# One decoder layer on one core: prompt choice, sample scores and time steps in one block, and a reworked first norm

## The chip, the core and the metric

The kernel runs on one NeuronCore of a Trainium2 chip. TensorE (PE) multiplies, VectorE (DVE), ScalarE (ACT) and GpSimd (POOL) work element by element, SyncE (SP) and the other queues issue transfers (DMA). All data is float32. The metric is device microseconds of one execution; lower is better.

## The reference, cut to what matters

One inference step of one decoder layer for 256 prompt tokens and 8 sample tokens (one new token each, 1,024 past positions). The two groups share all weights, so most products have 264 columns.

1. x is normed (RMSNorm over 1,024 channels) and multiplied with one input matrix. Its columns give z (2,048), x/B/C (4,096), the time steps dt (32), q, k, v, the indexer's queries, key and weights, and two gates of 1,024.
2. x/B/C goes through a causal convolution of width 4 and SiLU, and then, with dt, through a chunked state-space scan (prompt) or one recurrent step (samples). `dt = softplus(dt_raw + bias)`, `A = -exp(a_log)`.
3. The indexer scores every earlier position, `sum_h w_h relu(q_h k)`, and each query keeps the best: 64 of 256 in the prompt, 256 of 1,025 for a sample. Attention with a relative bias runs over those.
4. Both branches are gated, projected and added to x; then a product-key expert layer (PEER) follows, which picks 128 single-neuron experts for each token and gathers their rows.

## The kernel before

The input projection is cut into 81 tiles of 128 output channels. `Projection.multiply` computes one: eight pairs of multiplications of a 128x128 piece of weights with 264 columns of the normed x (`xn`), so 16 on PE. `Projection.load` issues the weights of tile n (512 KB) into one of `WSLOTS = 4` buffers on SP's queue, `evacuate` takes the result out of one of two PSUM banks on ACT, `convolve` (DVE) does the convolution of an x/B/C tile two tiles later, `tails` (POOL) keeps its last rows. The tiles are dealt out to the blocks that follow each other, to fill PE beside other work. A block ends when all engines have ended their part of it; then semaphores are cleared behind a barrier. The order is written out by hand, and each engine follows its own list. In time order:

- `norm_in` (lines 96 to 141) loads x, the constants (`cst`, `cx`: identity, ones, masks, epsilon), the norm's weights and four weight tiles, all on SP. ACT squares x, PE sums over channels with a matrix of ones from `cst`, ACT takes the root, DVE inverts it and writes `xn` in eight products.
- `project_attention` computes tiles 0 to 16 (q, k, v, indexer, dt); POOL loads 36 of the samples' 64 pages of indexer keys.
- `prepare_attention` norms q and k, builds the bias table, turns v; 6 tiles lie beside it. SP stores `o_k` and waits for the store.
- `choose_prompt` scores the prompt (16 steps: PE, then ReLU on ACT, then a weighted sum on DVE) and finds the best 64 by eight rounds of MAX8 and MATCH_REPLACE8 on two score tiles; 8 tiles beside it, the last 4 with nothing else on PE.
- `score_sample` scores the samples: PE copies queries out, DVE puts them on a diagonal (`iqd`), PE turns the pages and multiplies, ACT copies and rectifies, PE weighs, DVE copies to `negs`. No tile lies beside it.
- `attend_prompt` has 32 steps of prompt attention; in each, DVE also does one round of the samples' choice (MAX8 and MATCH_REPLACE8 over 1,025 scores). 38 tiles lie beside it: z tiles 14 and 15, all 32 x/B/C tiles and 4 gates. So six steps carry two tiles.
- `time_steps` computes dt, its decays and `ex` (values spread to channels by 16 multiplications with a 1 MB matrix `spread`); 2 tiles.
- `attend_sample` runs the samples' attention and the recurrent states (`SampleState`: 1 MB loaded and stored for each sample). The key phase has 16 visits; in each of the first 12 PE turns pages, multiplies, and spreads B and C (`ss_pb`, `ss_pc`) for DVE's update of half a state. Then comes the softmax, and the value phase with two visits for each sample. `LastGates` multiplies the last 10 gate tiles, with three weight buffers of its own and one PSUM bank: two ahead of the softmax, eight in the value phase, one for each sample.
- Then `ssd_chunk` twice, `merge` and `peer`, which the change leaves alone.

Of the kernel before, what the change touches and what calls it, by code (L numbers as in the profile page):

```python
# [19 lines left out]
P = 128  # L20
# [5 lines left out]
T = TP + TS  # L26
# [22 lines left out]
Z0 = N_ATT + 1  # L49
XBC0 = Z0 + N_Z  # L50
GATE0 = XBC0 + N_XBC
N_LAST = 10
# [10 lines left out]
CX_N = 256  # L63
# [8 lines left out]
class Kept:  # L72
# [5 lines left out]
            "d_relbh", "d_spread", "d_state", "d_uv", "d_w_ab", "d_w_in", "d_w_out", "d_wq", "d_xT")  # L78
# [15 lines left out]


def norm_in(nc, k):

    with ExitStack() as ctx:
        sem = signals(nc, ctx)
        xsq, g1, rms = tensors(nc, ctx, n1_xsq=(P, KD, T), n1_g=(P, KD), n1_rms=(P, T))  # L100
        ps = ctx.enter_context(nc.psum_tensor("n1_ps", [P, 512], F32))
        x_loaded, c_loaded, squared, summed, rooted, inverted, done = (sem(n) for n in (
            "n1_x", "n1_c", "n1_sq", "n1_sum", "n1_root", "n1_inv", "n1_done"))
        block = ctx.enter_context(nc.Block())

        @block.sync
        def _(sp):
            sp.dma_start(k.xT[:], k.d_xT[:]).then_inc(x_loaded, 16)
            sp.dma_start(k.cst[:], k.d_cst[:]).then_inc(c_loaded, 16)
            sp.dma_start(k.cx[:], k.d_cx[:]).then_inc(c_loaded, 16)  # L110
            sp.dma_start(g1[:], k.d_g1[:]).then_inc(c_loaded, 16)
            for n in range(WSLOTS):
                k.proj.load(sp, n)
            sp.wait_ge(c_loaded, 48)

        @block.scalar
        def _(act):
            act.wait_ge(x_loaded, 16)
            act.activation(xsq[:], k.xT[:], ACT.Square).then_inc(squared, 1)
            act.wait_ge(c_loaded, 48)  # L120
            act.wait_ge(summed, 1)
            act.activation(rms[:], ps[:, 0:T], ACT.Sqrt, scale=1.0 / D_MODEL, bias=k.eps).then_inc(rooted, 1)

        @block.tensor
        def _(pe):
            pe.wait_ge(c_loaded, 48)
            pe.wait_ge(squared, 1)
            for c in range(KD):
                mm = pe.matmul(ps[:, 0:T], k.ones, xsq[:, c, :], start=c == 0, stop=c == KD - 1)
            mm.then_inc(summed, 1)  # L130

        @block.vector
        def _(dve):
            dve.wait_ge(rooted, 1)
            dve.reciprocal(rms[:], rms[:]).then_inc(inverted, 1)
            dve.wait_ge(inverted, 1)
            dve.wait_ge(c_loaded, 48)
            for c in range(KD):
                dve.scalar_tensor_tensor(out=k.xn[:, c, :], in0=k.xT[:, c, :], scalar=g1[:, c:c + 1],
                                         in1=rms[:], op0=ALU.mult, op1=ALU.mult).then_inc(done, 1)  # L140
            dve.wait_ge(done, KD)


class Projection:
# [30 lines left out]
    def multiply(self, pe, n):  # L175
# [4 lines left out]
        for c in range(KD):  # L180
            mm = pe.matmul(self.ps[:, n % BANKS, 0:T], self.w[:, n % WSLOTS, c * P:(c + 1) * P],  # L181
                           self.k.xn[:, c, :], start=c == 0, stop=c == KD - 1)
        mm.then_inc(self.multiplied, 1)

    def evacuate(self, act, n):
# [3 lines left out]
        if n < XBC0:  # L189
            act.activation(k.zs[:, n - Z0, :], ps, ACT.Silu).then_inc(self.evacuated, 1)  # L190
        elif n < GATE0:
            s = (n - XBC0) % WSLOTS
            if n - XBC0 >= WSLOTS:

                act.wait_ge(self.convolved, n - XBC0 - WSLOTS + 1)
                act.wait_ge(self.saved, n - XBC0 - WSLOTS + 1)
# [5 lines left out]
        i = n - WSLOTS - XBC0  # L202
        if 0 <= i < KC:
# [3 lines left out]
    def convolve(self, dve, n):  # L207

        i = n - 2 - XBC0
        if not 0 <= i < KC:  # L210
            return
        s, cv = i % WSLOTS, self.cv[:, i % WSLOTS, :]

        dve.wait_ge(self.evacuated, i + XBC0 + 1)
# [15 lines left out]
    def tails(self, pool, n):  # L230

        i = n - XBC0
        if not 0 <= i < KC:
            return
        s = i % WSLOTS
# [64 lines left out]
def project_attention(nc, k):  # L300


    with ExitStack() as ctx:
        sem = signals(nc, ctx, "pr_")
        table, = (sem("table"),)
        block = ctx.enter_context(nc.Block())
# [3 lines left out]
        def _(sp):  # L310
            with sp.Fori(1, N_ATT // WSLOTS) as i:
# [5 lines left out]
            for n in range(N_ATT, Z0 + WSLOTS):  # L317
                pj.load(sp, n)

        @block.tensor  # L320
        def _(pe):
            for n in range(WSLOTS):
                pj.multiply(pe, n)
# [12 lines left out]
        def _(act):  # L336
            act.dma_start(pj.cw[:], k.d_cw[:]).then_inc(pj.c_loaded, 16)
# [4 lines left out]
            act.dma_start(k.hot[:], k.d_hot[:]).then_inc(k.tables_loaded, 16)  # L342
            with act.Fori(0, N_ATT // WSLOTS) as i:
# [6 lines left out]
            act.wait_ge(pj.evacuated, N_ATT + 1)  # L350

# [9 lines left out]
def prepare_attention(nc, k, tiles):  # L361

    with ExitStack() as ctx:
# [7 lines left out]
         stored, doubled, copied_table) = (sem("pa_" + n) for n in (  # L371
             "sq", "sum", "root", "inv", "normed", "turned", "copied", "tab", "tabout", "spread",
             "stored", "dup", "tabcp"))
# [5 lines left out]
        def _(sp):  # L379
            sp.dma_start(k.ikd[0:HD, :], k.misc[0:HD, :]).then_inc(doubled, 16)  # L380
            sp.dma_start(k.ikd[HD:P, :], k.misc[0:HD, :]).then_inc(doubled, 16)
            sp.dma_start(k.o_ik[:], k.misc[0:HD, :]).then_inc(stored, 16)
            sp.dma_start(k.o_v[:], k.att[:, V0:V0 + 2, :]).then_inc(stored, 16)
# [12 lines left out]
            sp.dma_start(k.o_k[:], k.att[:, K0:K0 + 2, :]).then_inc(stored, 16)  # L396
            sp.wait_ge(spread, 16)
            sp.wait_ge(doubled, 32)
            sp.wait_ge(stored, 48)
# [75 lines left out]
def choose_prompt(nc, k, tiles):  # L475

    TAIL = 4
    with ExitStack() as ctx:
        sem = signals(nc, ctx)
        r, iw = tensors(nc, ctx, cp_r=(P, 4, TP), cp_iw=(P, 2, IH))  # L480
        score, = tensors(nc, ctx, cp_score=(P, 2, TP))
        top, = tensors(nc, ctx, cp_top=(P, 2, 8))
        ps = ctx.enter_context(nc.psum_tensor("cp_ps", [P, 4, 512], F32))
        weighed, multiplied, rectified, added, cut, found, replaced, masked, final = (sem("cp_" + n) for n in (
            "w", "mm", "relu", "add", "cut", "max", "rep", "mask", "final"))
        block = ctx.enter_context(nc.Block())
        steps = [(i, h) for i in range(2) for h in range(IH)]
        width = lambda i: P * (i + 1)

        share, tail = shares(tiles[:-TAIL], len(steps)), tiles[-TAIL:]  # L490

# [6 lines left out]
        def _(pe):  # L498
# [9 lines left out]
            for tile in tail:  # L508
                k.proj.multiply(pe, tile)

        @block.scalar
        def _(act):
# [9 lines left out]
            for tile in tail:  # L522
                k.proj.evacuate(act, tile)

        @block.vector
        def _(dve):
            dve.tensor_scalar(iw[:], k.mnat[:, :, IW_P:IW_P + IH], IH ** -0.5, None, ALU.mult).then_inc(weighed, 1)
# [14 lines left out]
            for step in range(SEL_P // 8):  # L542
                for i in range(2):
# [8 lines left out]
                    dve.match_replace(s, top[:, i, :], s, LOW).then_inc(replaced, 1)  # L552
            for i in range(2):
# [3 lines left out]
            for tile in tail:  # L557
                k.proj.convolve(dve, tile)

        @block.gpsimd  # L560
        def _(pool):
            for tile in tiles:
                k.proj.tails(pool, tile)
            for i in range(2):
# [4 lines left out]
                                   pattern=[[-1, P]], channel_multiplier=1).then_inc(cut, 1)  # L569
            for i in range(2):  # L570
# [5 lines left out]


def score_sample(nc, k):

    with ExitStack() as ctx:  # L580
        sem = signals(nc, ctx, "cs_")
        ikt, iqd, r, wsel = tensors(
            nc, ctx, cs_ikt=(P, 2, 512), cs_iqd=(P, TS, TS * IH), cs_r=(TS * IH, NKS),
            cs_wsel=(TS * IH, TS))
        tr = ctx.enter_context(nc.psum_tensor("cs_tr", [P, 2, 512], F32))
        small = ctx.enter_context(nc.psum_tensor("cs_small", [P, 512], F32))
        ps = ctx.enter_context(nc.psum_tensor("cs_ps", [P, 3, 512], F32))
        cleared, spread, diag, weighed, turned, copied, scored, rectified, summed, read = (sem(n) for n in (
            "clr", "spread", "diag", "w", "turn", "copy", "score", "relu", "sum", "read"))
        block = ctx.enter_context(nc.Block())  # L590

        ik = k.paged[:].rearrange("p (a d) -> p a d", d=HD)

        @block.tensor
        def _(pe):

            for h in range(IH):
                pe.matmul(small[:, h * TS:(h + 1) * TS], k.selhi if h % 2 else k.sello,
                               k.att[:, IQ0 + h // 2, TP:T], start=True, stop=True)
# [1662 lines left out]
```

## Time and profile before

| what | us |
|---|---|
| median of 3 runs (lowest to highest) | 1476.19 (1475.57 to 1476.94) |
| the profiled execution's own time; its span | 1481.15; 1479.5 |
| `norm_in`, to the first projection tile | 0 to 22.9 |
| `project_attention` | 22.9 to 86.4 |
| `prepare_attention` | 86.4 to 124.25 |
| `choose_prompt` and `score_sample` | 124.25 to 186.3 |
| `attend_prompt` | 186.3 to 379.2 |
| `time_steps` | 379.2 to 399.2 |
| `attend_sample` | 399.2 to 548.3 |
| the rest | 548.3 to 1479.5 |

The times of blocks are read from the trace; each begins with its first instruction. In the rows below, a group of the timeline begins with its start and its duration (us), then engine, line, operation, output<-inputs, forms and how often; the bracket holds the idle time of that engine before it and what ended it. A row marked x16 covers a run of 16 instructions. A row of the windows view holds the stretch, its length, the busy time of PE, PEld (loads of weights into PE), DVE, ACT and POOL with their instructions in brackets, PEclk (the granted TensorE clock as a share of full speed), the busy share of the DMA engines and the GB/s that they moved.

### The profile page before, as it was taken

To read this page: it belongs to the slowest core of one execution; us is meant where nothing else is said; L and a number is where in the kernel's file an instruction comes from. 1 tells how busy PE (TensorE), PEld (TensorE's weight loads), DVE (VectorE), ACT (ScalarE), POOL (GpSimd) and SP (SyncE) were. 2 spreads that over 40 slices of the span, in tenths; PEclk is the share of its full clock that TensorE was granted. 3 is DMA by queue.
4 is the path that set the end of the run, shared out by engine and by line. 5 is a ranking of instruction groups with operands and counts; after the bars stand their busy time and mean duration, and the time that the engine had idled before them with its cause. 6 is when DMAs were issued, how large, how long until landed. Compare 5 with 4: busy or idle time off the path is not lost. (4 is left out here: it accounts for less than half of the span.)

```text
span 1479.5 us, 17316 instructions
## 1 busy us (share of the span) xinstructions
PE 1257.2 (85%) x4988; PEld 770.5 (52%) x4988; DVE 857.2 (58%) x2345; ACT 580.8 (39%) x1542; POOL 383.9 (26%) x510
## 2 busy tenths in 40 slices
PE   5997899999677878889989999877778777777776
PEld 4876578777555557758867555322223222222221
DVE  1044369998284334551116867878965667776444
ACT  1153237878383404320004444343343333333343
POOL 1320012222021110010002445443534334333341
PEclk8998999999796889899999999999999999999999
DMA  4563123334289462123337999999999999999995
GB/s 151 172 214 99 58 93 122 111 103 148 100 285 327 149 232 76 29 72 117 112 127 297 420 421 421 421 420 421 421 422 421 421 421 420 421 421 419 421 413 238
DMA packets 80185, 391.26 MB, mean 264 GB/s; under 512 B 13432, under 2 KB 23192, under 8 KB 43744
## 3 DMA queue, kind: packets, MB, share of 16 engines
q0 software_dynamic: 43104, 287.92, 47.5%
q1 hardware_dynamic: 36016, 100.68, 19.9%
q10 hardware_dynamic: 976, 1.61, 0.3%
q8 instruction: 39, 0.64, 0.2%
q14 instruction: 50, 0.41, 0.1%
HBM read 378.43 MB, written 11.60 MB: 264 GB/s over the span
## 5 line engine op out<-in xcount | busy, mean ns | idle before, releaser
L2039 DVE CUSTOM_DVE_ANT_0 pe_uv<-pe_uv,pe_hnat 128x1024 f32<-128x1024 f32 x264 | 322.9, 1223 | 195.4 <-DMA pe_uv<-d_uv,pe_idx 180.5
L1899 POOL DMA_INDIRECT pe_uv<-d_uv,pe_idx x256 | 268.0, 1047 | 398.4 <-PE pe_acc L1776 184.3
L1776 PE MATMUL pe_ph<-pe_uv,pe_dg 128*128 128x512 f32 x512 | 253.0, 618 | 69.8 <-ACT pe_dg L1843 69.8
L1776 PE MATMUL pe_acc<-pe_uv,pe_dg 128*128 128x512 f32 (+1 forms) x544 | 257.8, 610 | 49.3 <-ACT pe_dg L1843 49.3
L181 PE MATMUL pi_ps<-xn,pi_w 128*128 128x264 f32 x944 | 228.3, 399 | 9.5 <-PEq L87 9.5
L1776 PEld LDWEIGHTS pe_ph<-pe_uv,pe_dg 128*128 128x128 f32 x512 | 87.0, 189 | 235.3 <-ACT pe_dg L1843 173.1
L181 PEld LDWEIGHTS pi_ps<-xn,pi_w 128*128 128x128 f32 x944 | 183.5, 198 | 42.8 <-issue 11.3
L1837 ACT ACTIVATE pe_gl<-pe_a 128x1 f32<-128x1 f32 x264 | 53.4, 202 | 379.0 <-DVE pe_a L2039 378.5
L1776 PEld LDWEIGHTS pe_acc<-pe_uv,pe_dg 128*128 128x128 f32 (+1 forms) x544 | 93.7, 184 | 205.0 <-ACT pe_dg L1843 118.2
L1843 ACT ACTIVATE pe_dg<-cst,pe_w 128x128 f32<-128x128 f32 x256 | 102.7, 401 | 8.3
L1840 ACT ACTIVATE pe_w<-pe_gl,pe_gw 128x1 f32<-128x1 f32 x256 | 75.4, 295 | 8.3
L1715 PE MATMUL pq_ps<-hN,pq_w 128*128 128x264 f32 x256 | 61.7, 399 | 6.4 <-DMA pq_w<-d_wq 6.4
L957 PE MATMUL mg_pa<-Y,mw_w 128*128 128x264 f32 x256 | 60.5, 401 | 0.0
L1715 PEld LDWEIGHTS pq_ps<-hN,pq_w 128*128 128x128 f32 x256 | 50.1, 197 | 19.1 <-DMA pq_w<-d_wq 6.8
L957 PEld LDWEIGHTS mg_pa<-Y,mw_w 128*128 128x128 f32 x256 | 50.5, 198 | 10.1 <-issue 1.0
L226 DVE SCALAR_TENSOR_TENSOR pi_cv<-pi_raw,pi_cw,pi_cv 128x288 f32<-128x288 f32 x96 | 49.8, 519 | 3.4
L1260 DVE SCALAR_TENSOR_TENSOR ss_h<-ss_pb,ss_dtx,ss_h 128x128 f32<-128x128 f32 x128 | 35.0, 343 | 24.9 <-ACT ss_h L1247 17.0
L1617 ACT ACTIVATE mg_sq<-xT 128x264 f32<-128x264 f32 x8 | 3.4, 423 | 109.4 <-DVE xT L1647 109.4
L244 POOL COPY pi_tail_p<-pi_raw 128x3 f32<-128x3 f32 x32 | 12.0, 374 | 132.1 <-ACT pi_raw L198 132.1
L330 PE MATMUL pi_ps<-xn,pi_w 128*128 128x264 f32 x192 | 42.9, 386 | 0.0
L296 POOL DMA_DIRECT2D paged<-d_cik x50 | 26.8, 536 | 58.2 <-issue 58.2
L276 PE MATMUL lg_ps<-xn,lg_w 128*128 128x264 f32 x160 | 40.0, 406 | 1.7 <-DMA lg_w<-d_w_in 1.1
(296 smaller groups left out, 1655.9 us busy)
## 6 DMA issues: line engine op xcount, KB each, us to landing
pi_w<-d_w_in SPq DMA_DIRECT2D x71, 512.0 KB, 3.5
mw_w<-d_w_ab SPq DMA_DIRECT2D x24, 512.0 KB, 3.7
ss_h<-d_state SPq DMA_DIRECT2D x8, 1024.0 KB, 6.9
o_ssm_s<-ss_h SPq DMA_DIRECT2D x8, 1024.0 KB, 7.0
pq_w<-d_wq SPq DMA_DIRECT2D x16, 512.0 KB, 7.7
paged<-d_ck POOLq DMA_DIRECT2D x40, 128.0 KB, 3.3
lg_w<-d_w_in SPq DMA_DIRECT2D x10, 512.0 KB, 6.4
paged<-d_cv POOLq DMA_DIRECT2D x32, 128.0 KB, 4.9
```

What stands on the lines that cost most here:

```text
L181: mm = pe.matmul(self.ps[:, n % BANKS, 0:T], self.w[:, n % WSLOTS, c * P:(c + 1) * P], self.k.xn[:, c, :], start=c == 0, stop=c == KD - 1)
L226: dve.scalar_tensor_tensor(out=cv, in0=self.raw[:, s, j:j + CV], scalar=self.cw[:, i, j:j + 1], in1=cv, op0=ALU.mult, op1=ALU.add).then_in ...
L276: mm = pe.matmul(self.ps[:, 0:T], self.w[:, s, c * P:(c + 1) * P], self.k.xn[:, c, :], start=c == 0, stop=c == KD - 1)
L330: mm = pe.matmul(pj.ps[:, s % BANKS, 0:T], pj.w[:, s, c * P:(c + 1) * P], k.xn[:, c, :], start=c == 0, stop=c == KD - 1)
L957: mm = pe.matmul(out, self.w[:, i % self.RING, c * P:(c + 1) * P], rhs(c), start=c == 0 and piece < 2, stop=c == KD - 1 and piece != 1)
L1715: mm = pe.matmul(qps[:, n % BANKS, 0:T], w[:, n % WSLOTS, c * P:(c + 1) * P], k.hN[:, c, :], start=c == 0, stop=c == KD - 1)
L1776: mm = pe.matmul(accs[n][0:m, 4 * half:4 * half + 4, :], lhsT, uv[:, r, D_MODEL + half * 512:D_MODEL + (half + 1) * 512], start=False, sto ...
L1837: act.activation(gl[:, r:r + 1], a[:, r:r + 1], ACT.Gelu_apprx_tanh).then_inc(gelued, 1)
L1840: act.activation(wt[:, r:r + 1], gl[:, r:r + 1], ACT.Copy, scale=g).then_inc(weighed, 1)
L1843: act.activation(out, mask, ACT.Copy, scale=wt[:, r:r + 1]).then_inc(diagonal, 1)
L1899: pool.indirect_dma_start(uv[:, r, :], None, k.d_uv[:], bass.IndirectOffsetOnAxis(ap=src, axis=0)).then_inc(gathered[r], 16)
L2039: dve.tensor_tensor_reduce(uv[:, r, 0:D_MODEL], uv[:, r, 0:D_MODEL], hnat[:, n, :], 1.0, 0.0, ALU.mult, ALU.add, a[:, r:r + 1]).then_inc(d ...
```

## The change

`norm_in` goes into `project_attention`. x comes in four parts, which DVE squares as they come; the ones are written on chip; ACT loads the square root's table early; `cx` and the norm's weights come on ACT's queue, and `cst` on SP's behind the first four weight tiles. The first tile's multiplications wait for `xn` piece by piece.

`choose_prompt`, `score_sample` and `time_steps` become one block, `choose`, with 7 tiles. The time steps' parts and the samples' diagonal lie between the rounds of the prompt's choice on DVE; `ex` comes from one multiplication with a small selection matrix in place of 16. Their inputs are loaded in `prepare_attention`, scratch space lies in the not yet written `gate`.

The tiles are dealt out anew: z and x/B/C in the order `COLUMNS`; 7 tiles in `prepare_attention` (before 6), 7 in `choose` (8, and 2 in `time_steps`), 34 in `attend_prompt` (38), one for each step and two behind, and 16 in `LastGates` (10): one behind each of the key phase's visits 3, 6, 9 and 12, two ahead of the softmax, ten in the value phase (two at the first and the fifth sample). The bias inputs of `attend_sample` are loaded in `attend_prompt`. The wait for the stores of `prepare_attention` goes to `attend_prompt`.

```diff
-N_LAST = 10
+N_LAST, N_KEYS = 16, 4
+COLUMNS = "z" * 7 + "x" * 4 + "z" * 3 + "x" * 28 + "z" * 6
...
 def project_attention(nc, k):
...
         def _(sp):
+            for i in range(PARTS):
+                sp.dma_start(k.xT[:, i * WIDE:(i + 1) * WIDE, :], k.d_xT[:, i * WIDE:(i + 1) * WIDE, :]
+                             ).then_inc(x_loaded[i], 16)
+            for n in range(WSLOTS):
+                pj.load(sp, n)
+            sp.dma_start(k.cst[:], k.d_cst[:]).then_inc(c_loaded, 16)
...
         def _(pe):
+            pe.wait_ge(filled, 1)
+            for c in range(KD):
+                if c % WIDE == 0:
+                    pe.wait_ge(squared, c // WIDE + 1)
+                mm = pe.matmul(sums[:, 0:T], one[:], xsq[:, c, :], start=c == 0, stop=c == KD - 1)
             for n in range(WSLOTS):
-                pj.multiply(pe, n)
+                pj.multiply(pe, n, (lambda c: pe.wait_ge(done, c + 1)) if n == 0 else None)
...
         def _(act):
+            act.dma_start(k.cx[:], k.d_cx[:]).then_inc(eps_loaded, 16)
+            act.dma_start(g1[:], k.d_g1[:]).then_inc(eps_loaded, 16)
+            act.wait_ge(filled, 2)
+            act.activation(warm[:, 1:2], warm[:, 0:1], ACT.Sqrt).then_inc(warmed, 1)
...
 def prepare_attention(nc, k, tiles):
...
+            sp.dma_start(k.ts["bias"], k.d_dtb[:]).then_inc(k.steps_loaded, 16)
+            sp.dma_start(k.ts["alog"], k.d_alog[:]).then_inc(k.steps_loaded, 16)
+            sp.dma_start(k.dskip[:], k.d_dskip[:]).then_inc(k.steps_loaded, 16)
...
-            sp.wait_ge(stored, 48)
...
+def choose(nc, k, tiles):
+    TAIL, STEPS = 3, SEL_P // 8
...
         def _(pe):
...
+            k.proj.multiply(pe, tail[0])
+            pe.wait_ge(rectified, len(steps))
...
+            k.proj.multiply(pe, tail[1])
...
+                if b == 1:
+                    pe.wait_ge(diag, TS)
+                if b:
+                    scores(b - 1)
+                if b == 5:
+                    pe.wait_ge(s_weighed, 2)
+                    pe.wait_ge(dA_ready, 1)
...
+            k.proj.multiply(pe, tail[2])
...
         def _(act):
...
+            act.wait_ge(abs_ready, 1)
+            act.activation(e, a, ACT.Exp, scale=-1.0).then_inc(e_ready, 1)
+            act.wait_ge(k.steps_loaded, 48)
+            act.activation(alog, alog, ACT.Exp).then_inc(alog_ready, 1)
+            k.proj.evacuate(act, tail[0])
+            act.wait_ge(u_ready, 1)
+            act.activation(l, u, ACT.Ln).then_inc(log_ready, 1)
+            k.proj.evacuate(act, tail[1])
+            for b in range(TS):
...
+                if b == 4:
+                    act.wait_ge(dA_ready, 1)
+                    act.activation(both[rows, TS:2 * TS], k.dA[rows, NP_:ALL], ACT.Exp).then_inc(both_dA, 1)
...
         def _(dve):
...
+            for step in range(STEPS):
...
+                for tile in beside[step]:
+                    k.proj.convolve(dve, tile)
+                if step == 1:
...
+                    dve.tensor_tensor(e, a, e, ALU.mult).then_inc(ratio, 1)
+                if step == 4:
+                    dve.wait_ge(spread, 1)
+                    for b in range(TS):
...
 def attend_prompt(nc, k, tiles):
...
-        share = shares(tiles, N) + [[]] * LAG_O
+        share = shares(tiles[:-2], N) + [[], tiles[-2:-1], tiles[-1:]]
...
+            sp.dma_start(k.as_hot, k.d_hots[:]).then_inc(k.bias_loaded, 16)
+            sp.dma_start(k.as_rel, k.d_relbh[:]).then_inc(k.bias_loaded, 16)
...
 def attend_sample(nc, k):
...
-        after = [[]] * VK + [[0, 1]] + shares(range(2, N_LAST), TS)
+        after = ([[(t - 3) // 3] if t % 3 == 0 and 3 <= t < 3 + 3 * N_KEYS else [] for t in range(VK)]
+                 + [[N_KEYS, N_KEYS + 1]] + shares(range(N_KEYS + 2, N_LAST), TS))
...
+                if visit - NG < gates.SLOTS:
+                    gates.load(sp, visit - NG)
...
-        weights_at = [VK + NG + 1 if t == VK else VK + NG + 2 * (t - VK) for t in turn]
+        weights_at = [t + NG + 1 if t <= VK else VK + NG + 2 * (t - VK) for t in turn]
...
                 if n % 2 == 1 and n // 2 < EARLY:
                     ssd.spread(pe, n // 2)
+                if n % 2 == 1 and n // 2 < VK:
+                    for g in after[n // 2]:
+                        gates.multiply(pe, g)
...
-        ends = [Z0, Z0 + 6, Z0 + 14, END - BANKS, END]
+        ends = [FIRST0, FIRST0 + 7, FIRST0 + 14, END]
```

## Rows read from the trace of the kernel before

**Rows 1.** Stages by windows view: us, busy us of each engine, PEclk, DMA share, GB/s:
```profile
124.25:186.30 62.05, 56.29 (x264) 39.53 (x264) 20.66 (x81) 14.42 (x36) 1.16 (x4) 0.89 0.21 68
...
186.30:379.20 192.90, 188.47 (x880) 149.91 (x880) 165.61 (x385) 139.04 (x290) 40.70 (x112) 0.98 0.34 112
...
379.20:399.20 20.00, 15.37 (x68) 13.34 (x68) 3.74 (x15) 7.54 (x13) 0.00 (x0) 0.76 0.18 57
...
399.20:477.60 78.40, 55.29 (x524) 41.46 (x524) 47.93 (x306) 45.45 (x128) 17.16 (x32) 0.78 0.88 314
```

**Rows 2.** Timeline of the start:
```profile
5.92 1.96 ACT L119 ACTIVATE n_xsq<-xT 128x2112 f32<-128x2112 f32 x1 [3.74 <-DMA xT<-d_xT]
...
8.03 6.80 PE L129 MATMUL n_ps<-n_xsq,cst 128*128 128x264 f32 x16 [8.03 <-ACT n_xsq L119]
...
14.92 1.28 ACT L122 ACT_TABLE_LOAD   x1 [7.03 <-PE n_ps L129]
...
16.73 1.80 DVE L135 RECIPROCAL n_rms<-n_rms 128x264 f32<-128x264 f32 x1 [16.73 <-ACT n_rms L122]
...
18.57 3.32 DVE L139 SCALAR_TENSOR_TENSOR xn<-xT,n_g,n_rms 128x264 f32<-128x264 f32 x8
...
22.86 7.33 PE L181 MATMUL pi_ps<-xn,pi_w 128*128 128x264 f32 x21 [8.03 <-PEq L87]
```

**Rows 3.** Timeline, one of 13 projection tiles that repeat: ACT's copy behind each:
```profile
43.45 0.39 ACT L346 ACTIVATE att<-pi_ps 128x264 f32 x1 [3.17 <-PE pi_ps L330]
```

**Rows 4.** SP's own waits at the end of `prepare_attention`: us, times, longest:
```profile
SPq L399 <- DMA o_k<-att: 1.7, 1, 1.7
```

**Rows 5.** Timeline of `choose_prompt` and `score_sample`:
```profile
147.85 0.28 DVE L550 MAX8 cp_top<-cp_score 128x8 f32<-128x128 f32 x1
...
159.42 0.42 DVE L555 TENSOR_SCALAR negp<-cp_score 128x128 f32<-128x128 f32 x2
...
166.87 1.97 PE L611 MATMUL cs_ps<-cs_ikt,cs_iqd 64*64 64x512 f32 x4
...
180.62 0.22 PE L613 MATMUL cs_ps<-misc,cs_iqd 64*64 64x1 f32 x2
...
184.01 1.34 DVE L661 COPY negs<-cs_ps 8x512 f32<-8x512 f32 x3 [18.90 <-PE cs_ps L631]
```

**Rows 6.** Timeline of `attend_prompt`: two steps of its first half, and the end:
```profile
227.65 0.41 DVE L222 TENSOR_SCALAR pi_cv<-pi_raw,pi_cw,pi_cb 128x288 f32<-128x288 f32 x1
...
228.09 1.63 DVE L226 SCALAR_TENSOR_TENSOR pi_cv<-pi_raw,pi_cw,pi_cv 128x288 f32<-128x288 f32 x3
...
228.19 0.48 PE L721 MATMUL ap_psl<-att 64*128 64x128 f32 x2
...
232.87 0.41 DVE L222 TENSOR_SCALAR pi_cv<-pi_raw,pi_cw,pi_cb 128x288 f32<-128x288 f32 x1
...
232.92 0.49 PE L721 MATMUL ap_psl<-att 64*128 64x128 f32 x2
...
375.87 2.05 PE L742 MATMUL ap_pso<-ap_pt,vnat 128*128 128x128 f32 x8 [3.10 <-ACT ap_pt L805]
```

**Rows 7.** Waits in the key phase of `attend_sample`: us, times, longest:
```profile
PE as_tr L1403 <- DMA paged<-d_ck: 6.6, 2, 3.7
...
ACT ss_h L1247 <- DMA ss_h<-d_state: 5.6, 2, 3.8
...
PE as_pl L1379 <- DMA as_rel<-d_relbh: 4.5, 1, 4.5
```

**Rows 8.** Timeline of one visit of the key phase:
```profile
412.79 0.65 PE L1237 MATMUL ss_pc<-cst,xbc 128*128 128x128 f32 x4 [0.96 <-DVE ss_y L1268]
```

**Rows 9.** Timeline of the value phase: two gates:
```profile
498.66 3.80 PE L276 MATMUL lg_ps<-xn,lg_w 128*128 128x264 f32 x16
...
505.55 3.83 PE L276 MATMUL lg_ps<-xn,lg_w 128*128 128x264 f32 x16 [1.08 <-DMA lg_w<-d_w_in]
```

**Rows 10.** Waits in the value phase:
```profile
PE as_pl L1437 <- DMA paged<-d_cv: 3.1, 2, 2.5
```

More of the change, by code:

```diff
@@ L93, in signals @@
     return sem
[L96 to L141, printed above, removed]
 class Projection:
@@ L230, in tails @@
     def tails(self, pool, n):
[L232 to L233 removed]
+        if n not in X_AT:
             return
+        i = X_AT[n]
         s = i % WSLOTS
@@ L305, in project_attention @@
         table, = (sem("table"),)
+        xsq, g1, rms, one, warm = tensors(nc, ctx, n1_xsq=(P, KD, T), n1_g=(P, KD), n1_rms=(P, T), n1_one=(P, P),
+                                          n1_warm=(P, 2))
+        sums = ctx.enter_context(nc.psum_tensor("n1_ps", [P, 512], F32))
+        PARTS, WIDE = 4, KD // 4
+        x_loaded = [sem(f"n1_x{i}") for i in range(PARTS)]
+        c_loaded, eps_loaded, squared, summed, rooted, inverted, done, filled, warmed = (sem("n1_" + n) for n in (
+            "c", "eps", "sq", "sum", "root", "inv", "done", "one", "warm"))
         block = ctx.enter_context(nc.Block())
@@ L350, in _ @@
             act.wait_ge(pj.evacuated, N_ATT + 1)
+        @block.vector
+        def _(dve):
+            dve.memset(one[:], 1.0).then_inc(filled, 1)
+            dve.memset(warm[:], 1.0).then_inc(filled, 1)
+            for i in range(PARTS):
+                dve.wait_ge(x_loaded[i], 16)
+                xi = k.xT[:, i * WIDE:(i + 1) * WIDE, :]
+                dve.tensor_tensor(xsq[:, i * WIDE:(i + 1) * WIDE, :], xi, xi, ALU.mult).then_inc(squared, 1)
+            dve.wait_ge(rooted, 1)
+            dve.reciprocal(rms[:], rms[:]).then_inc(inverted, 1)
+            dve.wait_ge(inverted, 1)
+            dve.wait_ge(eps_loaded, 32)
+            for c in range(KD):
+                dve.scalar_tensor_tensor(out=k.xn[:, c, :], in0=k.xT[:, c, :], scalar=g1[:, c:c + 1],
+                                         in1=rms[:], op0=ALU.mult, op1=ALU.mult).then_inc(done, 1)
         @block.gpsimd
@@ L483, in choose_prompt @@
         ps = ctx.enter_context(nc.psum_tensor("cp_ps", [P, 4, 512], F32))
+        tr = ctx.enter_context(nc.psum_tensor("cs_tr", [P, 2, 512], F32))
+        small, cum, px = ps[:, 3, 0:256], ps[:, 3, 256:256 + 2 * NP_], tr[:, 0, 0:KI * 2 * TS]
         weighed, multiplied, rectified, added, cut, found, replaced, masked, final = (sem("cp_" + n) for n in (
             "w", "mm", "relu", "add", "cut", "max", "rep", "mask", "final"))
+        cleared, spread, diag, s_weighed, turned, copied, scored, s_rectified, summed, read = (
+            sem("cs_" + n) for n in ("clr", "spread", "diag", "w", "turn", "copy", "score", "relu", "sum", "read"))
@@ L486, in choose_prompt @@
+        x_ready, abs_ready, e_ready, alog_ready, u_ready, rest, inverted, ratio, log_ready = (
+            sem("ts_" + n) for n in ("x", "abs", "e", "alog", "u", "rest", "inv", "ratio", "log"))
+        log_out, dt_ready, dA_ready, both_dt, both_dA, each_ready, cumulated, widened, nac_ready, seg_ready, dec_exp, \
+            etot_ready, last = (sem("ts_" + n) for n in (
+                "lout", "dt", "dA", "bdt", "bdA", "each", "cum", "wide", "nac", "seg", "dexp", "etot", "last"))
         block = ctx.enter_context(nc.Block())
+        rows = slice(DT_P, P)
@@ L507, in _ @@
                     k.proj.multiply(pe, tile)
-            for tile in tail:
-                k.proj.multiply(pe, tile)
+            k.proj.multiply(pe, tail[0])
+            pe.wait_ge(rectified, len(steps))
+            for h in range(IH):
+                pe.matmul(small[:, h * TS:(h + 1) * TS], k.selhi if h % 2 else k.sello,
+                          k.att[:, IQ0 + h // 2, TP:T], start=True, stop=True)
+            pe.matmul(small[0:TS * IH, 128:128 + TS], k.iwsel, k.misc[:, TP:T], start=True, stop=True
+                      ).then_inc(spread, 1)
@@ L511, in _ @@
+            k.proj.multiply(pe, tail[2])
+            pe.wait_ge(s_rectified, 1)
+            for at, n in ((0, 512), (512, 512), (1024, 1)):
+                mm = pe.matmul(ps[0:TS, at // 512, 0:n], wsel[:], sr[:, at:at + n], start=True, stop=True)
+            mm.then_inc(summed, 1)
+            pe.wait_ge(each_ready, 1)
+            pe.matmul(px, k.half_of, k.ts["each"][rows, :], start=True, stop=True,
+                      tile_position=(DT_P, 0)).then_inc(widened, 1)
         @block.scalar
@@ L783, in _ @@
                     k.proj.convolve(dve, tile)
+            assert not any(t - 2 in X_AT for t in tiles[-2:])
             dve.wait_ge(replaced, N)
@@ L1462, in _ @@
                     ssd.fade(act, n // 2)
+                if n % 2 == 0 and n:
+                    for g in after[n // 2 - 1]:
+                        gates.evacuate(act, g)
             for g in after[VK]:
```

387 lines of the change are left out of this document (166 added, 221 removed).

## Prediction, made before the changed kernel ran

> **What bounds the kernel now.** I read the windows by stage first. Nothing after `attend_sample` is touched, so only the 548 us before it matter, and each stage there has its own limit. In `attend_prompt` PE is busy 188.5 of 192.9 us at a clock of 0.98, so a tile taken out of it is worth a tile. `time_steps` works 15.4 of its 20 us on PE, two tiles and a chain of small steps behind them. The key phase of `attend_sample` keeps the DMA engines 88% busy and PE only 55.3 of 78.4 us [rows 1]. Then I read the timeline of the start: the norm is one chain from engine to engine, and the first tile begins at 22.86 [rows 2]. A tile costs 3.56 us at the full clock (0.39 of copy and 3.17 of waiting between two copies) [rows 3]. Last came the waits, since the change moves stores, weights and tiles behind other waits [rows 4, 7, 10].
>
> The number of tiles stays 81. So a gain can only come from idle PE time, and the sum is taken along the chain of blocks: how much earlier or later does each one end than it would?
>
> **The start.** Before: the sum over channels begins at 8.03 and takes 6.80, the table load 1.28, root and hand-over 0.5, inversion 1.84, eight products 3.32, the barrier 0.97 [rows 2]. After, a quarter of x can be squared while the rest comes. All of x took until 5.92. A part's square is priced from the products, 0.415 for 264 columns, so 0.83 for 528. PE can begin between 3.0 (a quarter of the 5 us from issue to landing, plus 0.83) and 6.8 (all of x, plus 0.83); I take 4.5. Then 6.80 again for the sum, 0.1 + 0.5 + 1.84, and one product of 0.42, since PE follows piece by piece: the first tile begins at 14.2, which is 8.7 earlier (bounds 6.4 to 10.2). The constants behind the weights cost nothing: `cst` is first read 17 tiles or 60 us later; the weights that take its place in the queue have until 14.2, and what stood in that place before had landed by 8.0, or PE could not have begun. If that cover went, the first tile would wait for its weights. POOL's page loads and ACT's loads start earlier and have the same 60 us.
>
> The 1.28 of the table load is in this sum as the row has it. The Trainium skill, "ScalarE: Activation LUTs", section "What ACT_TABLE_LOAD costs", says that a change of table set costs about 2.66 us, 1.28 for the load and 1.38 for a drain. The row shows no drain: load and root end within 1.9 us of the load's beginning. By the page the start would gain 1.4 more, by the row it does not, and I stay with the row.
>
> **`prepare_attention`.** One more tile, 3.56; the wait for the store of `o_k`, 1.7 [rows 4], goes: 1.9 later (bounds 0.5, if the tile fills a wait of PE, and 3.6). The three added loads on SP stand ahead of the bias table's trip to memory; next late would be the weights of the fifth tile, and those wait for the first tile anyway.
>
> **`choose`.** Before, 62.05 + 20.0 = 82.05 [rows 1]. Up to the last prompt score nothing moves on PE (the same four tiles lie between), so DVE starts the rounds at 147.85 again, and eight rounds take 11.57, 1.45 each [rows 5]. The samples' diagonal now waits for five rounds (7.2), two convolutions (2.07 each, begin of the first to end of the last step [rows 6]) and four small steps of the time steps (1.4, estimated from 15 such in 3.74 us of DVE time [rows 1]); with 0.9 for the diagonal that is 161.4. PE has by then done two tiles and turned two pages and stands, at about 157.5, for 4 us. From the first sample score to the last took 166.87 to 180.84, 14.0 [rows 5]; begun at 161.4 it ends at 175.4, plus 1.5 for the cumulative sums and a table change on ACT in the middle, plus the last tile 3.56 (which hides ACT's rectifying, about 1.2 of the 3.2 between 180.84 and the copies at 184.01), plus 1.9 for the weighing: 182.4. From the copies' start to the next block took 186.3 - 184.0 = 2.3, and `ex` adds 0.4: 185.1. That is 1.2 earlier, and the 20.0 are gone: 21.2. Bounds: 16, if ACT's four further table changes at 1.28 all fall into the path; 25, if PE keeps its full clock through the 4 us (the first pages then go as fast as the last) and the diagonal comes a round earlier.
>
> **`attend_prompt`.** Four tiles fewer: 14.2. Against it stands DVE: in the first half PE's step takes 4.73 (228.19 to 232.92), DVE's step with a convolution 5.22 (227.65 to 232.87) [rows 6], and from the third step on each of 14 steps has one. That is 6.9 us in all, of which PE's two buffers hide some; between 0 and 6.9 I take 3.5. The two last tiles lie where PE waited 3.1 for ACT at the end [rows 6], which gives that back. The two bias loads at the head of SP's queue delay weights that are four tiles ahead, so nothing: -14.2 + 3.5 - 3.1 = -13.8 (bounds -17.3 and -7.3).
>
> **`attend_sample`** takes six more tiles, 21.4 on PE. Begin: PE no longer waits 4.5 for the bias inputs [rows 7], but the diagonal of queries and the first state come at their own time; between 0 and 4.5 I take 2.0. Key phase: a gate behind `ss_pc` fills the 0.96 that PE waits there [rows 8] and delays DVE by the rest, 2.6; three of them 7.8, the fourth lies in the 6.6 of waiting for pages. The delay is given back where states come late anyway, 5.6 [rows 7]. Their weights, 2.1 MB, are 6.7 us at 314 GB/s, against 12% of 78.4 = 9.4 us of idle DMA [rows 1]; I take 2 of it as lateness. Three of these loads go from SP's visits 13 to 15 to 4 to 6, and each later one waits on SP for the gate three before it, with pages and states queued behind; that gate is done by then, since SP comes to the visit only when PE has turned pages behind it. That is -2.0 + 7.8 - 5.6 + 2 = +2.2. Value phase: the second gate of the first sample is wanted at 502.4, when the first ends, but its weights are issued where those were that PE waited 1.08 for and got at 505.55 [rows 9]: 3.1 of waiting, less the 1.08. SP comes to those weights only when both visits of that sample are mixed, so this can't be earlier. Two more tiles 7.1, less 3.1 of waiting for pages that they fill [rows 10]: +6.0. In all 8.2 (bounds -0.5, which is the whole 4.5 at the begin, nothing for the key phase and 4.0 for the value phase; +24.5, with six whole tiles and the 3.1).
>
> **The sum.** -8.7 + 1.9 - 21.2 - 13.8 + 8.2 = -33.6. The profiled execution took 1481.15, so 1447.5 for such a one; the median lies 4.96 lower, at 1476.19, so 1442.6.
>
> **Rivals.**
> (a) The gates are paid in full. For it: in the key phase every engine waits for a chain through two buffers, and SP issues states, pages and gates in one order. Against it: 5.6 + 6.6 us of DMA waits lie there. `attend_sample` +24.5 in place of +8.2: 1458.9.
> (b) More goes: the full clock holds in `choose` (-3), PE's buffers hide DVE's pace (-3.5), and denser work in `attend_sample` saves part of the stretches at half clock that hold its clock at 0.78 (-4). Each has a row for it [rows 1, 6]; all together are less likely: 1432.
> (c) The start does not do what it says: x or the weights land so late in parts that nothing is gained, 1451.3. Against it: PE and DVE work in series there before, and the barrier goes in any case.
> (d) The other side: PE falls to the lower of its two clock levels in the first half of `attend_prompt`, since DVE now sets the pace and PE stops in each step. The same 16 multiplications took 6.80 in the norm and 3.56 later, so a tile would cost 3.24 more [rows 2, 3]: 16 tiles 52, 1495; it decides from ten tiles on. The Trainium skill, "TensorE: Matmul & The Clock Gate", section "A second HAM failure mode: psum-queue depth-cycling", says just this of a kernel whose matmul groups are parted by short waits on PSUM. Here the rows speak against it: PE would still be busy 4.73 of 5.22 us, and the clock was low where PE was busy 70% of the time, not at 98% [rows 1].
>
> **Chances and range.** Forecast 0.60, (a) 0.18, (b) 0.12, (c) 0.06, (d) 0.04. About 0.2% (3 us) is what a measurement can tell from no change: faster 0.96; of (d) one part in four ends near zero, same 0.01; slower 0.03. The range runs from 1430 to 1459: it holds the forecast's own bounds, nearly all of (c), half of (a) and two thirds of (b).
>
> **What would show it.** The first tile near 14.2; the block after `choose` some 21 us nearer to the end of `prepare_attention` than `attend_prompt` and `attend_sample` together were; `attend_prompt` near 179 us, with steps near 5.2 in its first half; the key phase 2 us longer, the value phase 6. The prediction is wrong if PE's clock falls outside the waits named, if ACT's table changes in `choose` hold up the pages, or if states and pages in the key phase come later by more than the gates take.

## The result, and the profile after

The changed kernel takes 1430.03 us (median of 4 runs, 1427.50 to 1433.12), before 1476.57 (4 runs): ratio 0.9677, 95% interval [0.9642, 0.9711]. On the median of the table above that is 1428.5, so 47.7 less where 33.6 were forecast; it lies just below the range. The profiled execution took 1433.12 with a span of 1431.5, so the span fell by 48.0.

To see where, I took the borders of the stages from the timelines. The first column is the forecast, the second the two profiled executions, the third means over three profiles a side: before, b1 and b2 below against after, b3 and b4, which differ from them in places of tiles and one small load (for the last row only the two of each side whose ring of expert rows lies where it lay).

| stage | forecast | profiled pair | means |
|---|---|---|---|
| start and `project_attention` | -8.7 | -7.8 | -8.1 |
| `prepare_attention` | +1.9 | 0.0 | +1.7 |
| `choose`, `attend_prompt` | -35.0 | -35.7 | -34.3 |
| `attend_sample`, key phase | +2.2 | -3.9 | -4.3 |
| softmax and value phase | +6.0 | +13.0 | +9.9 |
| `ssd_chunk` to the first gather | 0 | -3.5 | -0.1 |
| from the first gather to the end | 0 | -10.1 | -10.1 |
| sum | -33.6 | -48.0 | -45.3 |

Up to the first gather the means give -35.2, close to the forecast, though the two halves of `attend_sample` miss in opposite ways. The rest is the last row, in `peer`, which no line of the diff touches.

Windows of the kernel after, by stage (columns as in [rows 1]): `choose`, `attend_prompt`, key phase, softmax and value phase, and the gathers.

```profile
116.49:176.16 59.67, 52.76 (x254) 36.56 (x255) 32.17 (x114) 22.70 (x54) 3.44 (x16) 0.92 0.20 63
176.16:355.73 179.57, 176.27 (x816) 136.71 (x816) 157.54 (x369) 132.31 (x277) 37.50 (x100) 0.99 0.32 104
355.73:430.05 74.32, 60.45 (x588) 47.71 (x589) 48.26 (x306) 47.47 (x133) 16.78 (x32) 0.95 0.93 332
430.05:514.02 83.97, 67.31 (x383) 48.17 (x382) 22.66 (x116) 19.37 (x53) 13.27 (x25) 0.90 0.54 183
...
751.00:1387.60 636.60, 535.67 (x1308) 223.63 (x1306) 457.50 (x1167) 255.18 (x797) 270.61 (x255) 0.99 1.01 424
```

The same windows view of the kernel before, from its first gather to its 256th:

```profile
788.90:1434.90 646.00, 535.05 (x1308) 221.98 (x1306) 457.81 (x1167) 255.38 (x797) 267.07 (x256) 1.00 1.01 419
```

The engines do the same work in both; the DMA engines are busy throughout (1.01), and move 424 GB/s in place of 419. `attend_prompt` kept its clock, and the key phase, which had 0.78 [rows 1], has 0.95.

Timeline of the start after (answers to [rows 2]):

```profile
4.10 1.46 DVE L344 TENSOR_TENSOR n_xsq<-xT 128x528 f32<-128x528 f32 x2 [2.92 <-DMA xT<-d_xT]
...
4.95 6.43 PE L298 MATMUL n_ps<-n_xsq,n_one 128*128 128x264 f32 x16 [4.95 <-DVE n_xsq L344]
...
7.25 0.71 DVE L344 TENSOR_TENSOR n_xsq<-xT 128x528 f32<-128x528 f32 x1 [0.54 <-DMA xT<-d_xT]
...
11.48 0.48 ACT L327 ACTIVATE n_rms<-n_ps,cx 128x264 f32<-128x264 f32 x1 [8.15 <-PE n_ps L298]
...
14.47 2.10 PE L139 MATMUL pi_ps<-xn,pi_w 128*128 128x264 f32 x4 [3.09 <-DVE xn L350]
```

PE's sum begins at 4.95 while the last part of x is squared only at 7.25, and the first tile begins at 14.47 (forecast 14.2).

### The profile page after: what moved, and what is told of

Its sections match the earlier page's. It is cut to its first block and busy times, and to the rows that moved or that the text cites. A ratio compares the mean times of both kernels' runs of the same rounds, so it can differ in the third digit from the quotient of the medians.

```text
span 1431.5 us, 17196 instructions
## 1 busy us (share of the span) xinstructions
PE 1239.8 (87%) x4958; PEld 755.6 (53%) x4958; DVE 859.9 (60%) x2353; ACT 577.3 (40%) x1542; POOL 386.1 (27%) x510
## 3 DMA queue, kind: packets, MB, share of 16 engines
q0 software_dynamic: 43104, 287.92, 48.4%
## 5 line engine op out<-in xcount | busy, mean ns | idle before, releaser
L1878 POOL DMA_INDIRECT pe_uv<-d_uv,pe_idx x256 | 271.6, 1061 | 385.0 <-PE pe_ph L1755 178.6
L139 PE MATMUL pi_ps<-xn,pi_w 128*128 128x264 f32 x848 | 205.2, 398 | 3.1 <-DVE xn L350 3.1
L139 PEld LDWEIGHTS pi_ps<-xn,pi_w 128*128 128x128 f32 x848 | 163.1, 196 | 32.0 <-issue 4.7
L234 PE MATMUL lg_ps<-xn,lg_w 128*128 128x264 f32 x256 | 65.3, 411 | 7.8 <-DMA lg_w<-d_w_in 6.6
L234 PEld LDWEIGHTS lg_ps<-xn,lg_w 128*128 128x128 f32 x256 | 50.6, 203 | 20.0 <-DMA lg_w<-d_w_in 8.3
L202 POOL COPY pi_tail_p<-pi_raw 128x3 f32<-128x3 f32 x32 | 6.8, 212 | 138.2 <-ACT pi_raw L156 138.2
```

Source lines behind the costliest of these rows:

```text
L234: mm = pe.matmul(self.ps[:, 0:T], self.w[:, s, c * P:(c + 1) * P], self.k.xn[:, c, :], start=c == 0, stop=c == KD - 1)
L1878: pool.indirect_dma_start(uv[:, r, :], None, k.d_uv[:], bass.IndirectOffsetOnAxis(ap=src, axis=0)).then_inc(gathered[r], 16)
```

## Experiments

Every ratio is to the kernel before on the same chip. Without an edit of its own, a kernel is the changed one.

**b1 to b4: the gathers.** `CX_N` goes from 256 to 272 in the diff. `cx` lives to the end, so all that is allocated behind it moves by 64 bytes in each partition: the ring of expert rows `pe_uv` goes from byte 110,272 to 110,336. b1 is the kernel before, unchanged; the others:

```diff
# b2, in the kernel before
-CX_N = 256
+CX_N = 272
# b3, in peer
-        uv, hnat, ... = tensors(nc, ctx, pe_uv=(P, RING, 2 * D_MODEL), ...
+        _, uv, hnat, ... = tensors(nc, ctx, pe_pad=(P, 16), pe_uv=(P, RING, 2 * D_MODEL), ...
# b4, in prepare_attention, and d_spread among the inputs
+            sp.dma_start(k.spare[:], k.d_spread[:, 0:16]).then_inc(k.steps_loaded, 16)
```

> The kernel before, unchanged. The part behind attend_sample took 931.2 us in its profiled execution and 917.5 in that of the changed kernel, though no line of it differs: about 2.4 in the two ssd blocks, 1.2 up to the first gather and 9.4 in the gathers of the expert rows (646.0 against 636.6 us from the first to the last of 256, 421 against 427 GB/s). Theory 'execution': the gathers' rate differs from one execution to the next whatever the kernel, so this one lies anywhere between 636 and 646 us. Theories 'ring' and 'table' (the place of the ring in SBUF, the place of the expert table in DRAM): 646 again, within 2.

> The kernel before with one constant changed: the table cx is 272 columns wide in place of 256, its new columns zero and unread. All that is allocated behind it in SBUF, the ring of expert rows included, then lies 64 bytes further, where the changed kernel has it. Theory 'ring': the gathers take about 636.6 us and the kernel about 1466, 0.993 of before. Theories 'table' and 'execution': no difference from before by more than the runs scatter, ratio 1.000, gathers as in the run of the unchanged kernel.

> The changed kernel with 64 unused bytes in each partition ahead of the ring of expert rows, so that the ring lies at the same place relative to 128 bytes as in the kernel before. Theory 'ring': the gathers take 646 us again and the kernel about 1439.5, 0.975 of before. Theories 'table' and 'execution': as the changed kernel, about 1430, 0.968.

> The changed kernel with the input d_spread (1 MB) put back among its inputs; only 8 KB of it are loaded, into a tile of 64 bytes a partition that nobody reads, beside the other small loads of prepare_attention. Theory 'table': the expert table lies where it lay before, the gathers take 646 us again and the kernel about 1439.5, 0.975 of before. Theories 'ring' and 'execution': about 1430, 0.968; the tile lies in SBUF that the ring later covers, so the ring's place is unchanged.

Measured: b1 0.9987 [0.9973, 1.0001], b2 0.9926 [0.9901, 0.9951], b3 0.9734 [0.9713, 0.9756], b4 0.9687 [0.9664, 0.9710]. The gathers in the view of the ring's tile (duration of one in ns, lowest, median and highest; first and last start), in b2, b3 and the changed kernel:

```profile
L1899 POOL DMA_INDIRECT pe_uv<-d_uv,pe_idx x256: 942/944/3291, 783.7 to 1421.2; - x128
```
```profile
L1878 POOL DMA_INDIRECT pe_uv<-d_uv,pe_idx x256: 942/947/3337, 751.7 to 1397.3; - x128
```
```profile
L1878 POOL DMA_INDIRECT pe_uv<-d_uv,pe_idx x256: 939/944/3299, 751.0 to 1387.6; - x128
```

So 637.5, 645.6 and 636.6 us; b1 took 646.0 and b4 636.7. A wider table in the old kernel takes the gain, a pad in the new one gives it back, and the 1 MB input does nothing: theory "ring". The pad of b3 moves the tiles allocated behind the ring by 64 bytes too; no run moved the ring alone, but 265.6 of the 270.7 MB of the stretch before lie on the gathers' queue.

**c1 to c4: parts of the change.**

```diff
# c1
-N_LAST, N_KEYS = 16, 4
+N_LAST, N_KEYS = 14, 4
# c2
+N_LAST, N_KEYS = 12, 0
# c3
-        PARTS, WIDE = 4, KD // 4
+        PARTS, WIDE = 1, KD
# c4, in choose: the diagonal (DVE), the sums (PE), the exponent (ACT)
-                if step == 4:
+                if step == 1:
-                if b == 5:
+                if b == 7:
-                if b == 4:
+                if b == 6:
```

> The changed kernel with two gate tiles moved back from the value phase to attend_prompt (14 last gates in place of 16; no sample has two any more, two of 32 steps carry two tiles again). Theory 'late weights': the value phase is 9.9 us longer than before in the mean of three profiles each, though its two more tiles are only 7.5 of multiplication; the rest is the second gate of the first sample, which waits 3.7 for its weights and then runs at the lower clock (6.9 in place of 3.8), and later gates whose weights come late in turn. Then the value phase falls by 9 to 13, attend_prompt grows by 7.1, and the kernel takes 2 to 6 us less than the changed one. Rival 'a tile is a tile': the value phase falls by 7.5, attend_prompt grows by 7.1, and the time is that of the changed kernel within 1 us.

0.9649 [0.9617, 0.9681], 1425.2 us. The interval overlaps that of the changed kernel, so I read the stages (d2, below, is clear of it in time). The value phase fell by 13.8 (83.97 to 70.2), `attend_prompt` grew by 6.9. PE in the value phase of the changed kernel, and then of c1:

```profile
450.69 3.73 PE L234 MATMUL lg_ps<-xn,lg_w 128*128 128x264 f32 x16
458.08 6.86 PE L234 MATMUL lg_ps<-xn,lg_w 128*128 128x264 f32 x16 [3.67 <-DMA lg_w<-d_w_in]
```
```profile
457.98 3.73 PE L234 MATMUL lg_ps<-xn,lg_w 128*128 128x264 f32 x16
461.63 1.06 PE L1413 MATMUL as_pl<-paged,as_pt 128*16 128x256 f32 x16
```

The second gate of the first sample is gone, and its wait and its slow run with it: "late weights".

> The changed kernel without gates in the key phase: 12 last gates, four more tiles in attend_prompt. Theory 'hidden': in the key phase the four gates lie in waits for states and pages, so it stays at 73 to 74 us from the first bias product to the end of the last score product, within 2; attend_prompt grows by 4 x 3.55 = 14.2, and the kernel takes 12 to 16 us more than the changed one. The prediction's size for the key phase (each gate delays VectorE by 2.6, and 5.6 of the 7.8 are given back): it falls by some 4 us with its lateness of weights, so 10 more. Rival (a), the gates are paid in full: it falls by 15, the time does not change.

0.9735 [0.9703, 0.9767], 1436.33 us. The key phase took 66.1, so four gates cost 7.4 (against the mean of three profiles) to 8.2 (against the changed kernel's) of their 14.9 on PE; they are neither hidden nor paid in full. This is one profile, and the ten kernels that have the four gates took between 71 and 76 there, so the cost is known only to some 2 us. `attend_prompt` grew by 11.2, not 14.2.

> The changed kernel with x loaded in one transfer and squared in one instruction. Theory 'parts': about half of the 8 us that the start gained comes from squaring behind the first part; all of x takes until about 6, one square of 2112 columns 3.3, so TensorE's sum begins at 9.3 in place of 4.95, and the first tile begins at about 18.5 in place of 14.5: 4 us more. Rival 'weights decide': the first tile waits for its weights behind x anyway, and nothing is lost.

0.9711 [0.9672, 0.9750]. Timeline of c3:

```profile
6.33 2.36 DVE L344 TENSOR_TENSOR n_xsq<-xT 128x2112 f32<-128x2112 f32 x1 [5.15 <-DMA xT<-d_xT]
8.83 5.44 PE L298 MATMUL n_ps<-n_xsq,n_one 128*128 128x264 f32 x16 [8.83 <-DVE n_xsq L344]
```

PE's sum begins 3.9 later and takes 1.0 less, since it no longer waits for parts; the root begins at 14.38 against 11.48, and the first tile at 17.37 against 14.47. The parts are worth 2.9 of the start's 8; the time alone could not show it.

> The changed kernel with the samples' diagonal on VectorE behind the second round of the prompt's choice in place of the fifth, and the two waits for the time steps two samples later in the loop of sample scores. Theory 'on the path': TensorE stands 4.5 us for that diagonal (from 149.0 to 153.55), and the loop of sample scores decides when the block ends; the diagonal is then done at about 147.5, the first scores begin at about 149.5 to 150, and the block ends 3 to 4 us earlier; the kernel takes 3 to 4 us less. Rival 'rounds decide': the block ends with VectorE's rounds and the time steps behind them, and nothing is gained.

0.9667 [0.9629, 0.9704], 1425.03 us; the interval overlaps that of the changed kernel, so here too the stage tells: `choose` took 54.3 in place of 59.67. PE in the changed kernel and in c4, from the samples' first pages to the first scores:

```profile
147.97 1.04 PE L559 MATMUL cs_tr<-cst,paged 128*128 128x128 f32 x8
153.55 1.92 PE L548 MATMUL cp_ps<-cs_ikt,cs_iqd 64*64 64x512 f32 x4 [4.54 <-DVE cs_iqd L676]
```
```profile
145.44 1.04 PE L559 MATMUL cs_tr<-cst,paged 128*128 128x128 f32 x8
147.00 1.08 PE L548 MATMUL cp_ps<-cs_ikt,cs_iqd 64*64 64x512 f32 x4 [0.52 <-ACT cs_ikt L607]
```

The wait for the diagonal is gone (4.0 less between the two rows), and the first products behind it take 1.08 in place of 1.92, at a granted clock of 1.00 in place of 0.52: "on the path".

**d1: where the first gates' weights are loaded.** On top of c2:

```diff
-                if visit - NG < gates.SLOTS:
-                    gates.load(sp, visit - NG)
+                if VK - gates.SLOTS <= visit < VK:
+                    gates.load(sp, visit - VK + gates.SLOTS)
```

> The kernel of c2 (no gates in the key phase, 12 last gates) with the loads of the first three gates' weights back at the visits 13 to 15 where the kernel before had them, in place of 4 to 6. Theory 'place of the weights': without gates the key phase takes 66.1 us from the first state's load to the end of the last score product, 12 less than before (78.1); about 4 of that is its begin (no wait for the bias inputs, bias products at the full clock), and the other 8 come from 1.5 MB of weights that no longer stand between the last pages: before, TensorE waited 2.9 and 3.7 for those pages, fell to the lower clock and did the last products at it. Then the key phase takes 71 to 74 us here, with waits of several us for pages near its end, and the kernel 4 to 8 more than c2. Rival 'begin alone': the whole 12 come from a denser begin that keeps the clock and the transfers going; the key phase stays at 66, within 2.

0.9759 [0.9718, 0.9801], 1442.19 us; the interval overlaps c2's, but the key phase took 72.6 against 66.1. Waits of its key phase, us, times, longest, in c2 and in d1:

```profile
PE as_tr L1376 <- DMA paged<-d_ck: 2.5, 2, 1.9
```
```profile
PE as_tr L1376 <- DMA paged<-d_ck: 5.6, 2, 2.9
```

Windows view of the last 7.5 us of the key phase, in before, d1 and c2:

```profile
470.00:477.60 7.60, 7.60 (x74) 4.90 (x72) 0.00 (x0) 1.19 (x2) 1.07 (x2) 0.50 1.03 360
432.70:440.20 7.50, 6.38 (x78) 4.81 (x78) 0.00 (x0) 1.20 (x2) 1.38 (x3) 0.67 1.03 370
423.40:430.80 7.40, 5.38 (x94) 3.69 (x94) 0.00 (x0) 1.74 (x4) 2.81 (x6) 1.00 0.86 276
```

Before and d1 do their last products at a lowered clock, c2 at the full one. So the place of these weights is worth 6.5 ("place of the weights"; one profile each); 5.2 remain for the begin (77.8, the mean of three profiles of before from the block's first instruction, to 72.6). That is a difference; no run changed the begin alone.

**d2 to e1: both gains together, and which places of the ring are slow.** d2 is c1 and c4 in one. d3, d4 and e1 are d2 with `pe_pad` of 64, 8 and 32 columns.

> The changed kernel with both edits that gained: the diagonal early (c4) and two gates back in attend_prompt (c1). If the two lie in different stages, their gains add: the block choose some 5 us shorter, the value phase 13 shorter and attend_prompt 7 longer, in all 9 to 11 us less than the changed kernel, about 0.961 of before. Rival: what one gains the other takes, as both end in the same late pages or states: 5 to 6 less, as each alone.

> d2 with 256 unused bytes ahead of the ring of expert rows, so that it begins at a multiple of 512 bytes in its partition; in the changed kernel it begins at 256 past such a multiple, in the kernel before at 192 past one. Theory '128': only the place relative to 128 bytes counts, so the gathers take 636.6 us as in d2 and the time is the same. Theory '512': larger multiples help further; the gathers take less than 634 us.

> d2 with 32 unused bytes ahead of the ring, which then begins 32 bytes past a multiple of 64. If each row's 8 KB in a partition is written in pieces that end at multiples of 64 or more, a start that is no multiple of 64 is at least as bad as one at an odd multiple of 64: gathers of 646 us or more, the kernel 9 us or more above d2. If only the odd 64 was bad, 637.

> d2 with 128 unused bytes ahead of the ring of expert rows, which then begins 128 bytes past a multiple of 256. The fast places so far (those of the changed kernel and of d3) are multiples of 256, the slow ones lie 192, 64 and 32 past one, so the runs do not tell which multiple is wanted. Theory '256': the gathers take 645 to 648 us as at the slow places, the kernel some 10 us more than d2. Theory '128': 636.6 as in d2, no difference.

d2: 0.9588 [0.9558, 0.9619], 1417.30 us, faster than both kernels, by ratio 13.1 less than the changed one; `choose` took 54.2 as in c4, and the value phase some 69, about as in c1: the gains add. d3 0.9608 [0.9576, 0.9639], d4 0.9694 [0.9654, 0.9733], e1 0.9656 [0.9604, 0.9708]. The gathers of d4 and of e1:

```profile
L1878 POOL DMA_INDIRECT pe_uv<-d_uv,pe_idx x256: 939/944/3356, 732.0 to 1379.9; - x128
```
```profile
L1878 POOL DMA_INDIRECT pe_uv<-d_uv,pe_idx x256: 939/944/3317, 738.9 to 1384.9; - x128
```

| ring begins, past a multiple of 256 bytes | gathers, us | kernels |
|---|---|---|
| 0 | 636.5 to 637.5 | after, b2, b4, c1 to c4, d1 to d3 |
| 32 | 647.9 | d4 |
| 64 | 645.6 | b3 |
| 128 | 646.0 | e1 |
| 192 | 646.0 | before, b1 |

d4 is slow like the odd 64, and e1 shows that a multiple of 128 is not enough. Of the places tried, those at a multiple of 256 are fast, and a multiple of 512 (d3) adds nothing.

## Why the prediction was right in direction and too small

**The step that failed** is its first: "Nothing after `attend_sample` is touched, so only the 548 us before it matter". The code there is not touched, but its addresses are. The term that it set to nothing measured -10.1 (9.4 to the last of 256 gathers, 0.7 behind it); b2 and b3 show the cause from both sides. With the ring at a slow place again (b3) the changed kernel has 0.9734, which is 1436.9 on the table's median and 39.3 less than before, a time inside the range. What the page of before showed, and I did not weigh, is that the gathers fill the DMA engines for 646 us, so that 1.5% on them is 9.4 us, more than the whole start gives.

That the means up to the first gather give -35.2 is in part luck: the key phase came out 6.5 below its term and the value phase 3.9 above it. It is luck too that rival (b), at 1432, lies nearest to the 1428.5 measured: the key phase apart, its terms did not come. And the range holds the bounds of the terms only one at a time; the low ones taken together are -52.5, or 1423.7.

The Trainium skill, "DMA: Bandwidth & Descriptors", section "How a descriptor splits into AXI transactions", says that a transaction must begin at a multiple of 256 bytes, and that a descriptor which does not begin at one has its first transaction begin at the boundary below. It tells this of what is read; here the place that is written was moved, and the runs show the same 256 there. They do not agree with its count of beats (32 bytes each) as a price: for a row of 8 KB that would be 262 in place of 256 at 192 past (+2.3%) and 257 at 32 past (+0.4%, both estimates by that page); measured were +1.5% and +1.8%. Why the price is nearly the same at every offset stays open.

**Start: right.** -8.1 against -8.7. The table load is gone from the path and the barrier with it; neither was undone alone. As to its price, the timeline of the changed kernel has one in `choose`, with ACT's steps 0.01 ahead of it and behind it:

```profile
138.33 0.94 ACT L590 ACTIVATE gate<-cp_ps 128x256 f32<-128x256 f32 x3 [0.17 <-PE cp_ps L526]
139.28 1.28 ACT L596 ACT_TABLE_LOAD   x1
140.57 0.26 ACT L596 ACTIVATE gate<-gate 128x72 f32<-128x72 f32 x1
```

By the Trainium skill, "ScalarE: Activation LUTs", section "What ACT_TABLE_LOAD costs", 1.38 of drain would come on top; these rows leave no room for it on either side of the load.

**`prepare_attention`: right** in the mean (+1.7 against +1.9), though single profiles of one kernel differ by as much.

**`choose`: right.** -22.4 against -21.2 in the profiled pair. PE stood 4.54 for the diagonal (forecast 4), the loop from there to the last score took 13.95 with the sums in it (15.5), and c4 shows that this wait was on the path. The merging itself was read from the traces, not undone.

**`attend_prompt`: right.** 179.57 (forecast 179). From its eleventh step on DVE sets the pace in the first half; two steps in the timeline:

```profile
240.05 0.48 PE L798 MATMUL ap_psl<-att 64*128 64x128 f32 x2
...
245.28 0.48 PE L798 MATMUL ap_psl<-att 64*128 64x128 f32 x2
```

5.23 a step, as in [rows 6] for DVE. Rival (d) did not come: the granted clock is 0.99 there. What the Trainium skill, "TensorE: Matmul & The Clock Gate", section "A second HAM failure mode: psum-queue depth-cycling", tells of short idle times between groups, cited beside that rival, is not seen in these steps.

**Key phase: two sizes wrong.** The gates cost 7.4 (four at some 2), not 7.8 - 5.6 + 2 = 4.2. Against that I booked 2 for the begin, which gave 5.2 (by difference; the wait of 4.5 [rows 7] is gone, and the bias products, below, take 2.06 in place of 3.99, at a granted clock of 1.00 in place of 0.50), and a loss for moved weights that was a gain of 6.5 (d1): before, 1.5 MB stood between the last pages at the end of the phase, and PE waited there and did its last products at 0.50 of the clock. -5.2 - 6.5 + 7.4 = -4.3, a sum that must come out, as its terms are differences between the same four times. The bias products in the timelines of before and after:

```profile
401.83 3.99 PE L1379 MATMUL as_pl<-as_p,as_rel 32*128 32x512 f32 x6 [4.49 <-DMA as_rel<-d_relbh]
```
```profile
355.77 2.06 PE L1351 MATMUL as_pl<-gate 32*128 32x512 f32 x6 [1.74 <-PEq L91]
```

**Value phase: two sizes too small.** The late second gate was foreseen (3.1; it waited 3.67). Not foreseen was that PE's clock is lowered behind that wait: the gate then took 6.86 in place of 3.83. Windows view over it:

```profile
458.00:464.90 6.90, 6.82 (x20) 5.04 (x23) 0.00 (x0) 0.00 (x0) 0.00 (x0) 0.55 0.02 7
```

The granted clock is 0.55, near the lower of its two levels (1.2 of 2.4 GHz). And three later gates waited 2.96 for weights, where I had let before's 1.08 go. Waits by the profile, after:

```profile
PE lg_ps L234 <- DMA lg_w<-d_w_in: 6.6, 4, 3.7
```

With the 6.0 of the forecast this makes 6.0 + 0.6 + 3.0 + 3.0 = 12.6 of the pair's 13.0. The clock did not fall behind every such wait: the same gate waited 4.21, 3.75 and 3.77 in b3, b4 and c3 and took 6.14, 5.52 and 5.51, but in c4 it waited 3.42 and took 3.83. And before, b1 and b2 took 70.6, 75.7 and 72.9 for this phase, so the pair's 13.0 lies above the means' 9.9.

Rival (b) expected denser work in `attend_sample` to keep the clock. In the key phase the clock was kept (0.95), but not by density: c2, without gates there, has 0.92, and d1, which differs from c2 in the place of three loads, 0.84. In the value phase more work came with a clock of 0.90, against 0.91 before. Rival (a) fell with c2, and rival (c) with the first tile at 14.47.

## What to carry to other kernels

An edit that widens a tile which lives on moves everything allocated behind it: before calling a later stage untouched, compare the start addresses of the tiles that a DMA-bound stage writes, and put a ring for gathers of such rows at a multiple of 256 bytes. Moving a load can be worth as much as moving work: ask what its transfer stood in front of in the old place. A tile put where its weights come late costs the wait and, where the clock is lowered behind it, up to as much again (3.67 and 3.03 here).

## What the runs showed of the hardware

Indirect gathers of 8 KB rows into SBUF took 636.5 to 637.5 us for 256 when the ring of buffers began at a multiple of 256 bytes in its partition, and 645.6 to 647.9 when it began 32, 64, 128 or 192 past one: nearly one price for the four offsets tried, not one that grows with the bytes. The number of packets and their bytes are the same (43,104 and 287.92 MB on the gathers' queue); that the place in SBUF and not that in DRAM matters is shown by b3, which moves nothing in DRAM.
